# A decoder step in float32: weight blocks multiplied half by half, and the output projection started before the samples' rows are ready

## What is computed

```python
def diff_output(o, subln, w_o, lambda_init):
    B, T = o.shape[:2]
    o = rmsnorm(o, subln) * (1.0 - lambda_init)
    return o.reshape(B, T, D_MODEL) @ w_o

for i in range(DEPTH):
    hp, hs = rmsnorm(xp, norm_mix[i]), rmsnorm(xs, norm_mix[i])
    ...                                   # the mixer: pool, conv or attention
    yp = diff_output(o, attn_subln[ic], attn_w_o[ic], lambda_init)    # prompt, layer 2
    ys = diff_output(os_, attn_subln[ic], attn_w_o[ic], lambda_init)  # samples, layer 2
    ...
    xp = xp + yp
    xs = xs + ys
    xp = xp + swiglu(rmsnorm(xp, norm_ffn[i]), ffn_w_gate[i], ffn_w_up[i], ffn_w_down[i])
    xs = xs + swiglu(rmsnorm(xs, norm_ffn[i]), ffn_w_gate[i], ffn_w_up[i], ffn_w_down[i])
```

## Time and profile before

| | us |
|---|---|
| runs before: median (lowest, highest) | 2272.67 (2272.19, 2276.53) |
| the profiled execution, own time | 2274.68 |
| its span, first to last instruction | 2272.7 |
| TensorE busy | 2109.4 (93% of the span) |
| VectorE busy | 1085.4 (48%) |
| ScalarE busy | 951.6 (42%) |
| GpSimd busy | 324.6 (14%) |

### The profile page before, as it was taken

The page is one execution under the profiler, slowest core; times in us unless marked ns, Lnnn a source line. Parts: engine busy times, 40 slices in busy tenths (PEclk is TensorE's granted clock), DMA queues, the critical chain, the costliest instruction groups (busy, mean ns, idle before and its releaser), DMA issues. The chain is left out here.

```text
span 2272.7 us, 41338 instructions
## 1 busy us (share of the span) xinstructions
PE 2109.4 (93%) x16880; PEld 2028.2 (89%) x16880; DVE 1085.4 (48%) x1448; ACT 951.6 (42%) x1278; POOL 324.6 (14%) x293
## 2 busy tenths in 40 slices
PE   2899999999889999999999858999999949999998
PEld 1899999999369999999999746999999939999998
DVE  5644443359955444433466744444432284444321
ACT  3444432255755343322677732443332235333221
POOL 4200000148921000001111121000001140000000
PEclk9999999999899999999999988999999969999999
DMA  4233333232012333323543332333323212333231
GB/s 135 71 87 90 92 90 94 85 102 84 19 29 87 93 92 92 88 86 95 143 119 97 107 117 84 91 92 92 92 84 91 77 47 84 92 92 92 86 105 51
DMA packets 345053, 201.51 MB, mean 89 GB/s; under 512 B 7465, under 2 KB 337481, under 8 KB 344932
## 3 DMA queue, kind: packets, MB, share of 16 engines
q1 hardware_dynamic: 341460, 193.21, 29.3%
q0 software_dynamic: 3504, 7.06, 1.1%
HBM read 193.51 MB, written 8.60 MB: 89 GB/s over the span
## 5 line engine op out<-in xcount | busy, mean ns | idle before, releaser
L901 ACT ACTIVATE w_hi<-raw 128x1024 fp32r<-128x1024 f32 (+1 forms) x332 | 344.7, 1038 | 1001.6 <-PE acc L484 999.7
L484 PE MATMUL acc<-xin_hi,w_hi 128*128 128x260 f32 x3456 | 702.7, 284 | 4.4 <-DVE w_lo L1233 3.8
L484 PE MATMUL acc<-xin_hi,w_lo 128*128 128x260 f32 x3456 | 697.5, 283 | 0.0
L484 PE MATMUL acc<-xin_lo,w_hi 128*128 128x260 f32 x3456 | 696.5, 283 | 0.0
L1233 DVE TENSOR_TENSOR w_lo<-raw,w_hi 128x1024 fp32r<-128x1024 f32 (+1 forms) x332 | 405.6, 1222 | 343.7 <-ACT w_hi L901 343.6
L484 PEld LDWEIGHTS acc<-xin_hi,w_hi 128*128 128x128 f32 x3456 | 534.6, 189 | 16.1 <-issue 11.7
L484 PEld LDWEIGHTS acc<-xin_hi,w_lo 128*128 128x128 f32 x3456 | 534.1, 189 | 0.0
L484 PEld LDWEIGHTS acc<-xin_lo,w_hi 128*128 128x128 f32 x3456 | 533.0, 189 | 0.0
L484 PE MATMUL acc<-h_hi,w_hi 128*128 128x260 f32 x1408 | 284.4, 283 | 0.0
L484 PE MATMUL acc<-h_hi,w_lo 128*128 128x260 f32 x1408 | 283.1, 282 | 0.0
L484 PE MATMUL acc<-h_lo,w_hi 128*128 128x260 f32 x1408 | 282.7, 282 | 0.0
(11 more groups left out here) (281 smaller groups left out, 1921.2 us busy)
## 6 DMA issues: line engine op xcount, KB each, us to landing
raw<-in_ffn_w_gate SPq DMA_DIRECT2D x88, 512.0 KB, 3.9
raw<-in_ffn_w_up SPq DMA_DIRECT2D x88, 512.0 KB, 3.9
raw<-in_ffn_w_down SPq DMA_DIRECT2D x64, 512.0 KB, 3.9
raw<-in_ffn_w_down SPq DMA_DIRECT2D x32, 384.0 KB, 3.4
raw<-in_attn_w_qkv SPq DMA_DIRECT2D x24, 512.0 KB, 4.0
raw<-in_conv_w_in SPq DMA_DIRECT2D x16, 512.0 KB, 4.0
raw<-in_conv_w_out SPq DMA_DIRECT2D x8, 512.0 KB, 4.1
in_mix<-in_cache_k SPq DMA_DIRECT2D x8, 512.0 KB, 3.8
```

Source lines behind the costliest of these rows:

```text
L484: last = pe.matmul(acc[:, b + h, 0:HALF], w[:, w_tile * P:(w_tile + 1) * P], v[:, h * HALF:(h + 1) * HALF], start=start and t == 0, stop=s ...
L901: act.activation(w_hi[n.slot(2)][:, 0:cols], raw[:, n.slot(4), 0:cols], ACT.Copy).then_inc(split_hi, 1)
```

## The change

It touches TensorE's program alone. `tile_products` now does all three products of the first half and then all three of the second, through a new function `half_products`; this holds for every weight block of the kernel. And ahead of the wait for `os_scaled`, the first halves of the output projection's units 0 and 1 are run, over all 8 slices; their second halves follow where the two whole units stood. Units 2 to 7 stay as they were but for the order inside a slice.

```diff
+            def half_products(m, h, w_tile, s, k_hi, k_lo, start, stop):
+
+                b = 2 * m.slot(2) + h
+                for t, (w, v) in enumerate(((w_hi[s], k_hi), (w_hi[s], k_lo), (w_lo[s], k_hi))):
+                    last = pe.matmul(acc[:, b, 0:HALF], w[:, w_tile * P:(w_tile + 1) * P],
+                                     v[:, h * HALF:(h + 1) * HALF],
+                                     start=start and t == 0, stop=stop and t == 2)
+                return last
+
             def tile_products(m, w_tile, s, k_hi, k_lo, start, stop):
 
-                b = 2 * m.slot(2)
-                for t, (w, v) in enumerate(((w_hi[s], k_hi), (w_hi[s], k_lo), (w_lo[s], k_hi))):
-                    for h in range(2):
-                        last = pe.matmul(acc[:, b + h, 0:HALF], w[:, w_tile * P:(w_tile + 1) * P],
-                                         v[:, h * HALF:(h + 1) * HALF],
-                                         start=start and t == 0, stop=stop and t == 2)
+                for h in range(2):
+                    last = half_products(m, h, w_tile, s, k_hi, k_lo, start, stop)
                 return last
...
                 last.then_inc(weighted, 1)
+                def half_unit(i, h):
+                    n, m = At(UNIT["w_o"] + i), At(TILE["w_o"] + i)
+                    for k in range(KT):
+                        last = half_products(m, h, k, n.slot(2), mix_hi[:, k, :], mix_lo[:, k, :], k == 0, k == KT - 1)
+                    return last
+
+                pe.wait_ge(split_lo, UNIT["w_o"] + 2)
+                pe.wait_ge(mix_lo_ok, MIX["attn"] + HEADS)
+                for i in range(2):
+                    half_unit(i, 0)
                 pe.wait_ge(os_scaled, 1)
                 pe.transpose(bank7[:, 0:R], os_tok[:], ident).then_inc(os_back, 1)
                 pe.wait_ge(mix_lo_ok, MIX["attn"] + 1 + HEADS)
-                for i in range(KT):
+                for i in range(2):
+                    half_unit(i, 1).then_inc(units_done, 1)
+                for i in range(2, KT):
                     unit(At(UNIT["w_o"] + i), At(TILE["w_o"] + i), mix_hi, mix_lo)
```

## The result

| us | before | changed |
|---|---|---|
| median (lowest, highest; runs) | 2273.50 (2272.19, 2276.53; 5) | 2261.45 (2260.63, 2264.95; 5) |
| profiled execution: own time, span | 2274.68, 2272.7 | 2261.45, 2259.5 |

The ratio is 0.9946, with a 95% interval of 0.9933 to 0.9959: 9 to 15 us faster, where 6.0 was forecast. Measured once more, beside other kernels, the changed kernel came to 0.9953 (0.9939 to 0.9966).

What follows compares the result with a forecast made beforehand. TensorE, busy 93% of the span, was taken to bound the kernel. Moved matmuls saved 5.77 us and the warm transpose 0.2, the rest 0: 2272.67 - 6.0 = 2266.7 us, range 2263.2 to 2271.6.

Steps and rivals of the forecast that it cites:

- part 4: Inside each slice of every product, 15,552 matmuls: the new order was taken to cost 0.
- Rival (e): Alternating banks hold the pace at 0.120 us a matmul; without that, some 120 us faster, near 2150; chance 0.03.
- Part 1: 48 first-half matmuls of units 0 and 1 fit ahead of the transpose, 1376.3 to 1382.1, with 1.9 us slack.
- Part 2: Second halves behind the transpose run cold, 7.68 us, saving 5.77 us; a warm transpose brings 0.2 us more.
- rival (a): Clock stays at 2.4 GHz over the shorter gap before the second halves: 1.9 us more saved, 2264.8; chance 0.10.
- Part 3: Unit 2's weights, which wait for unit 0, are covered by unit 1's second half, 0.3 us to spare: cost 0.
- (b): New order costs 0.1 to 0.3 ns a matmul everywhere, giving back 1.6 to 4.7 us: 2268.3 to 2271.4; chance 0.14.
- (c): Adding to a just-written bank is slower, 2.8 ns on 10,368 matmuls, 29 us: 2295.7; chance 0.08.
- (d): First halves meet a halved clock, or unit 2 waits for its split: 2 to 3 us lost; chance 0.07.

Runs made afterwards that it cites:

- the order alone: Kernel before with the half-by-half order inside each slice and no first halves ahead of the transpose: 2269.71 us against 2273.02, ratio 0.9983.
- banks in turn: Changed kernel with the same reads and weights, but the six matmuls of a slice writing to the two PSUM banks alternately: 2260.9 us, one run.
- fixed weights: Changed kernel whose whole units load the weights of their first 128 input channels for every slice, streamed reads unchanged: 2262.37 us, one run.
- alternating halves: Kernel before with the changed kernel's order of weights but halves switching at each matmul, nothing moved ahead of the transpose: 2272.01 us against 2273.02, ratio 0.9996.
- the early halves alone: Kernel before, old order in whole units, with only the first halves of output-projection units 0 and 1 ahead of the transpose: 2268.14 us, ratio 0.9978.
- the turned order: Changed kernel with the order of the two halves reversed at every second slice: 2260.21 us against 2273.52, ratio 0.9946.
- the two orders in one kernel: Changed kernel with halves first, first, second, first, second, second, but down units reversing halves every second slice: 2258.04 us against 2273.57, ratio 0.9933.

## Why the prediction was wrong

**The step that failed is part 4, the order inside each slice.** I put it at 0 and kept only a loss in the range. It is a gain: 1.4 us in each of four blocks by the traces, some 6 us in all, and 2 to 6 us by the run of the order alone. My bounds came from rows that differ in how banks follow each other, and these rows stream a column in 0.82 and 0.86 ns, while the products take 120 / 260 = 0.46 ns: another kind of matmul, which says nothing of half a nanosecond on this one. The bank has no part in the gain (the run with banks in turn), nor has the place of the weights (fixed weights), and the new order of weights alone doesn't bring it (alternating halves). The property that counts, where each streamed read starts, was not on my list, though the change alters its sequence throughout the 15,552 matmuls. By my own sign, a unit in the feed-forward blocks that moves by more than 0.01 us from 5.77, the prediction was wrong: 0.44 ns on 48 matmuls are 0.02 us. Rival (e) had noticed that 0.120 us is more than the cold pace explains; its cause, the alternating banks, is refuted.

**Part 1 was right.** The halves fit under VectorE's chain: a rest of 1.85 us was measured where 1.9 was worked out.

**Part 2, the clock, was right in kind and too simple.** I took "cold" from three waits of 3.7 us, and rival (a) was "stays warm". The same rest of about 3 us did both. It ended at full clock in the first trace of the changed kernel, which therefore won 7.5 us here, and with a fall in the second one (6.0 us: 20.53 - 14.53) and in that of the early halves alone (4.8). Eleven of the traces have both early halves and this unfilled rest. In two of them, the first one and the turned order's, tile 2 came 13.0 us after the transpose, in seven 14.3 to 14.5, and in two, the early halves alone and the two orders in one kernel, 15.7. So 6.0 us is what most of them won, but the number also leans on the one trace of before: in the other kernels whose wait is whole and unfilled the same distance was 20.6 to 21.7 us. The transpose was quicker, as forecast (0.33 us against 0.48), but the restart came only 0.14 us sooner behind it, and 0.03 us sooner after the samples' product (12.60 against 12.63), not 0.2.

**Part 3 was right.** Tile 0's evacuation was seen at 1385.50 and unit 2's weights were complete at 1387.87, 2.37 us later, as before; TensorE didn't wait for them.

**The sum.** The changed kernel's medians lie 12.1 and 11.2 us below before. The traces account for this: 6.0 or 7.5 us at the place, and 5 to 6 in the blocks. By the medians of the parts the sum is smaller, 4.9 us for the early halves and 3.3 for the order, 8.2 together. The intervals (3 to 7 and 2 to 6 us) cover the difference, so whether the parts merely add is not shown. Rivals (b) and (c), a small or a large cost of the order, are wrong in sign; (d) did not occur.

**What stays open** is the rule by which a sequence of start addresses makes a pace. Two runs change the reads alone, by 16 bytes or to one slice for all, and both move the block; every trace of one order has the same block to 0.1 us; they don't give a formula. No run changes the order of the weights and keeps the sequence of reads, so a small share of the weights' order, hidden by the reads, is not excluded.

## What to carry to other kernels

Where TensorE is the bound, weigh any reordering of its stream at all its matmuls, not only at the place that it is made for: by the traces, half a nanosecond on 15,000 matmuls was worth some 6 us here, about as much as the work put under the 7.7 us wait. Such a pace can't be read from a row of another kind of matmul; measure it as the length of a long stretch without waits, and try a few orders, since the best one differed between two kinds of unit. And count work moved under a wait by its own length; what the clock adds changes from one execution to the next.

## What the runs showed of the hardware

- The pace of one and the same matmul (128x128 weights, 260 columns, float32 parts, full clock) ranged from 379.8 to 386.5 us a block of 3168, that is by 2.1 ns in 120, over the orders and starts of reads that were tried. Moving every second read's start by 16 bytes alone made it 4.1 us longer. For one order the block is the same to 0.1 us from run to run.
- Writing to the bank just written cost nothing that a block shows (381.0 us in turn and not in turn). Nor did changing weights at 4 of 6 matmuls instead of 2 show a cost, though the reads changed with it (380.2 against 381.8 us with the early halves).
- With a rest of 1.85 us, a transpose and 0.85 us more, TensorE went on at 2.4 GHz in two traces of eleven. In the other nine the clock fell to 1.2 GHz at the restart or soon after it, and tile 2 came 1.3 to 2.7 us later.
- With 48 unused matmuls in the front of the 7.7 us wait the clock fell later, but was still half in most of the window from 1385 to 1390 (0.57), and the median didn't move (ratio 0.9999, 0.9990 to 1.0008).
